# First layer of a two-layer block: turns inside the tile stream, gates ahead of queries, dot products for the late adaptive rows, step sizes with tokens on the partitions

## The chip, the cores and the metric

The kernel runs on one core of a Trainium2 chip. The metric is the device time of one execution in microseconds. The engines are TensorE (PE, with its weight loads listed as PEld), VectorE (DVE), ScalarE (ACT), GpSimd (POOL) and SyncE (SP, which only issues DMAs here). All data are float32. A large product is made of three passes: every weight and every activation is split into a rounded high part and a low part (w_hi, w_lo, h_hi, h_lo), and PE adds hi x hi, hi x lo and lo x hi.

## The reference

One sequence of 512 tokens of width 1024 passes through two layers. The first has a neighbourhood attention and a state-space scan side by side; the second has a windowed attention. The change touches the first layer up to its attention. Cut to what matters:

```python
mod = silu(c) @ ada_w + ada_b                      # 6 rows of 1024: sh1, sc1, g1, sh2, sc2, g2
h = rms_norm(x, norm1_w) * (1 + sc1) + sh1         # hc likewise, from 256 context tokens
p = h @ w_in                                       # q, k, v (512 columns each), z, xs (512), B, C (256), dt (16)
q, k = axial_rope(q), axial_rope(k)
attn = neighbourhood_attention(q, k, v, kc, vc, rpb, rows)    # 8 heads, key windows and all context keys
dt = softplus(p_dt + dt_bias)                      # per token, 2 directions x 8 heads
xs, B, C = silu(depthwise_conv(...))               # three taps along the tokens
y = ssd_bidirectional(z, xs, B, C, dt, -exp(a_log), ...)      # needs xs and B with tokens on the partitions
x = x + g1 * (concat([attn, y]) @ w_out)
x = x + g2 * conv_glu(rms_norm(x, norm2_w) * (1 + sc2) + sh2, ...)
```

g1, sh2, sc2 and g2 are the late adaptive rows: they are needed only behind the attention and the scan.

## The kernel before, in words

Weights come in blocks of 1 MB (128 partitions x 2048). For each block SP issues the load into w_raw (two buffers), ACT copies it to w_hi (`high`), POOL subtracts to get w_lo (`low`, four instructions), and PE multiplies. The order on every engine is written out by hand, and semaphores join the engines.

The projection `p = h @ w_in` is a stream of 24 output tiles of 128 columns, two to a block, in the order of `KINDS`: k (tiles 0 to 3), v (4 to 7), xs (8 to 11), B (12, 13), C (14, 15), q (16 to 19), z (20 to 23). Tile n uses the PSUM bank n mod 4. PE may begin tile n when tile n-4 has been taken out of its bank (`tile_free`) and the block's low part is there (`lo_done`). The first 14 tiles have a second part for the 256 context tokens (`ctx_product`, plain float32, from w_raw, in banks 4 and 5). `lead` makes tiles 0 to 3 as the pieces of h become ready (`h_low`).

A k tile is rotated by DVE (`rope`), and the last of these is followed by a small row `brow` of the second layer's bias, made from bank 7 (`brow_done`, `brow_sb`). A v tile is copied out by DVE. For xs, B and C, ACT writes the middle tap, DVE adds the outer taps (`outer_taps`), and ACT takes silu; then the same for the context part. For q, DVE does five instructions that read the bank and two that add. For z, ACT takes silu. Beside each of the tiles 4 to 19 DVE multiplies one 1 MB chunk of ada_w by a value per partition and adds it to a sum (`add_ada1`, 128x2048); the chunks go through a ring of two, which ACT refills between its own instructions (`load_ada`, which waits until DVE has used a chunk).

Three serial parts stand between the last tile and the attention. PE sums the collected ada rows over the partitions (32 products with a column of ones, line 1223). The step sizes dt are worked out on 16 partitions x 768 columns by DVE and ACT (lines 1535 to 1541 and 1840 to 1854). Then 19 groups of four transposes (`TR`, line 1246) bring v, the context v, xs and B to tokens on the partitions: a v window is first gathered by DVE (line 1863), PE turns the group, and ACT and DVE copy groups out in turn (lines 1551 and 1881). After the eleventh group come the turns of dt and three small sums (lines 1234 to 1240). Then the attention begins: 16 steps G of scores for two heads (lines 494, 495), largest value and bias on DVE, exp on ACT, scaling on POOL (line 610), transposes on PE (line 504), copies on ACT (line 551), and weighing of v (line 515). Before it, POOL has made the low parts of blocks 12 and 13, the first two of the output projection.

## Time and profile before

| | |
|---|---|
| median of 3 runs | 1487.64 us (1487.33 to 1490.51) |
| the profiled execution's own time | 1488.21 us |
| its span, first to last instruction | 1486.4 us |
| PE busy | 1385.2 us (93%) |
| DVE, ACT, POOL busy | 603.2, 567.3, 636.4 us |
| mean granted TensorE clock over the span | 0.963 of full speed |
| share of the chain that ended last | PE 81%, DVE 6%, POOL 5%, issue 3%, ACT 3% |

The span leaves out 1.8 us of the execution. A busy PE is not a PE at its peak: the granted clock says in which stretches it ran at half speed. The chain of waits goes back from the last instruction to whatever released each one. Two matmul records of the profile stand for one plain float32 product, and one for a transpose or a rounded product.

### The profile page before, as it was taken

To read this page: it belongs to the slowest core of one execution; us is meant where nothing else is said; L and a number is where in the kernel's file an instruction comes from. 1 tells how busy PE (TensorE), PEld (TensorE's weight loads), DVE (VectorE), ACT (ScalarE), POOL (GpSimd) and SP (SyncE) were. 2 spreads that over 40 slices of the span, in tenths; PEclk is the share of its full clock that TensorE was granted. 3 is DMA by queue.
4 is the path that set the end of the run, shared out by engine and by line. 5 is a ranking of instruction groups with operands and counts; after the bars stand their busy time and mean duration, and the time that the engine had idled before them with its cause. 6 is when DMAs were issued, how large, how long until landed. Compare 5 with 4: busy or idle time off the path is not lost.

```text
span 1486.4 us, 17325 instructions
## 1 busy us (share of the span) xinstructions
PE 1385.2 (93%) x6360; PEld 1109.6 (75%) x6360; DVE 603.2 (41%) x1088; ACT 567.3 (38%) x856; POOL 636.4 (43%) x516
## 2 busy tenths in 40 slices
PE   8899997798778899999999989999979999999997
PEld 1788866686666678888888878755668888888885
DVE  2544578576852444434354243276151000001123
ACT  3512313463322534444333352377454222222331
POOL 0243354134642254444556654433523445445563
PEclk9899998899979899999999989999989999999999
DMA  9224552700012054454442242200211232322321
GB/s 394 93 101 162 214 188 98 170 1 1 1 57 113 29 220 176 184 211 178 189 155 99 88 168 85 86 1 1 70 44 57 85 113 85 107 90 85 113 85 57
DMA packets 26981, 165.49 MB, mean 111 GB/s; under 512 B 2688, under 2 KB 4992, under 8 KB 8496
## 3 DMA queue, kind: packets, MB, share of 16 engines
q1 hardware_dynamic: 24912, 150.10, 27.7%
q10 hardware_dynamic: 2016, 14.68, 2.8%
q8 instruction: 34, 0.56, 0.2%
q14 instruction: 19, 0.16, 0.0%
HBM read 162.64 MB, written 6.32 MB: 114 GB/s over the span
## 4 chain that ended last, share of the span: by engine, by line
PE 81%; DVE 6%; POOL 5%; issue 3%; ACT 3%; DMA 1%; SPq 0%; ACTq 0%; DVEq 0%; POOLq 0%
PE bank L271 48%; PE bank L335 9%; PE bank L312 5%; PE bank L1186 3%; PE bank L654 2%; PE bank L634 2%; PE bank L515 2%; POOL arena L832 1%; POOL w_lo L264 1%; PE bank L1163 1%; DMA w_raw<-w_dram 1%; POOL arena L834 1%; PE bank L1246 1%; PE bank L644 1%; PE bank L494 1%
## 5 line engine op out<-in xcount | busy, mean ns | idle before, releaser
L264 POOL TENSOR_TENSOR w_lo<-w_raw,w_hi 128x512 fp32r<-128x512 f32 x356 | 486.7, 1398 | 639.9 <-ACT w_hi L255 635.5
L271 PE MATMUL bank<-h_hi,w_hi 128*128 128x512 f32 x1120 | 445.2, 397 | 19.6 <-POOL w_lo L264 9.8
L271 PE MATMUL bank<-h_lo,w_hi 128*128 128x512 f32 x1120 | 440.3, 393 | 0.0
L271 PE MATMUL bank<-h_hi,w_lo 128*128 128x512 f32 x1120 | 439.8, 393 | 0.0
L255 ACT ACTIVATE w_hi<-w_raw 128x2048 fp32r<-128x2048 f32 x89 | 170.5, 1915 | 408.2 <-PE bank L271 189.5
L271 PEld LDWEIGHTS bank<-h_hi,w_hi 128*128 128x128 f32 x1120 | 213.5, 191 | 65.9 <-issue 13.7
L271 PEld LDWEIGHTS bank<-h_hi,w_lo 128*128 128x128 f32 x1120 | 212.9, 190 | 45.0
L271 PEld LDWEIGHTS bank<-h_lo,w_hi 128*128 128x128 f32 x1120 | 213.3, 190 | 43.6
L2036 DVE TENSOR_TENSOR arena<-arena,bank 128x512 f32 (+1 forms) x22 | 15.1, 688 | 210.2 <-PE bank L271 210.2
L1908 DVE TENSOR_TENSOR h_lo<-arena,h_hi 128x1024 fp32r<-128x1024 f32 x22 | 32.8, 1503 | 136.9 <-ACT h_hi L1585 125.4
L1753 DVE SCALAR_TENSOR_TENSOR arena<-bank,params,arena 128x511 f32<-128x511 f32 (+1 forms) x36 | 25.4, 705 | 147.2 <-ACT arena L1565 114.5
L335 PE MATMUL bank<-w_hi,h_hi 128*128 128x512 f32 x192 | 74.9, 390 | 4.7 <-POOL arena_rounded L232 3.3
L335 PE MATMUL bank<-w_hi,h_lo 128*128 128x512 f32 x192 | 75.0, 390 | 0.0
L335 PE MATMUL bank<-w_lo,h_hi 128*128 128x512 f32 x192 | 75.0, 390 | 0.0
L1744 DVE CUSTOM_DVE_ANT_0 ada_ring<-ada_ring,arena 128x1024 f32<-128x1024 f32 x48 | 62.2, 1331 | 0.0
L790 POOL TENSOR_SCALAR arena<-arena,small 128x256 f32<-128x256 f32 (+1 forms) x64 | 32.8, 532 | 55.6 <-DVE small L748 55.6
L610 POOL TENSOR_SCALAR arena<-arena,small 128x512 f32<-128x512 f32 x32 | 21.7, 692 | 73.2 <-DVE small L589 73.2
L1186 PE MATMUL bank<-arena,w_raw 128*128 128x256 f32 x224 | 50.5, 379 | 0.0
L1186 PEld LDWEIGHTS bank<-arena,w_raw 128*128 128x128 f32 x224 | 42.4, 190 | 6.9 <-issue 0.9
L634 PE MATMUL bank<-arena 128*128 128x256 f32 (+1 forms) x128 | 44.2, 458 | 3.5 <-DVE ada_ring L1992 2.6
L335 PEld LDWEIGHTS bank<-w_hi,h_hi 128*128 128x128 f32 x192 | 36.2, 188 | 13.4 <-issue 3.7
L312 PE MATMUL bank<-h_hi,w_hi 128*128 128x512 f32 x112 | 43.7, 390 | 0.0
(262 smaller groups left out, 1881.7 us busy)
## 6 DMA issues: line engine op xcount, KB each, us to landing
w_raw<-w_dram SPq DMA_DIRECT2D x92, 1024.0 KB, 4.8
ada_ring<-ada_dram SPq DMA_DIRECT2D x30, 1024.0 KB, 4.8
ada_ring<-ada_dram ACTq DMA_DIRECT2D x14, 1024.0 KB, 4.9
arena<-ada_dram SPq DMA_DIRECT2D x4, 1024.0 KB, 10.5
arena<-x_dram SPq DMA_DIRECT2D x2, 2048.0 KB, 11.4
bias_copies<-bias_rows SPq DMA_DIRECT2D x1, 4096.0 KB, 26.6
arena<-bias_copies SPq DMA_DIRECT2D x1, 3072.0 KB, 13.5
out_dram<-arena SPq DMA_DIRECT2D x8, 256.0 KB, 2.1
```

Of the source, the lines that this page charges most:

```text
L255: nc.scalar.activation(w_hi[b % 2][:], w_raw[b % 2][:], ACT.Copy).then_inc(hi_done, 1)
L264: last = nc.gpsimd.tensor_tensor(w_lo[b % 2][:, part], w_raw[b % 2][:, part], w_hi[b % 2][:, part], ALU.subtract)
L271: last = nc.tensor.matmul(bank[:, :], w[:, ft, k, :], x[:, k, :], start=k == first and m == 0, stop=k == final and m == 2)
L312: last = nc.tensor.matmul(ps[f][:, :], w[:, k, f, :], x[:, 2 * gslot + k, :], start=bank_free is not None and k == 0 and m == 0, stop=False)
L335: last = nc.tensor.matmul(ps[2 * t + h][:, :], x[:, slot + k, part], w[n][:, k, cols], start=start and m == 0, stop=stop and m == 2)
L515: last = nc.tensor.matmul(ps[7][:, 0:256], v, pt1[G % 2][:, kb, :], start=kb == 0, stop=kb == 3)
L634: nc.tensor.matmul(ps[u % 3][:, 0:128 * (hi - lo)], q2[:, 2 * g + hq // 2, t * 128:(t + 1) * 128], k2[:, g, hq % 2, lo * 128:hi * 128], st ...
L654: last = nc.tensor.matmul(ps[7][:, :], vtok2[:, lo + kb, g, :], pt2[:, G % 2, kb, :], start=kb == 0, stop=kb == hi - lo - 1)
L790: nc.gpsimd.tensor_scalar(prob2[:, u % 8, 0:w], prob2[:, u % 8, 0:w], row_inv[:, u % 16:u % 16 + 1], 1.0, ALU.mult, ALU.mult).then_inc(s[" ...
L1186: last = nc.tensor.matmul(ps[4 + n % 2][:, 0:CTX], raw[:, n % 2, k, :], HC[:, k, :], start=k == 0, stop=k == DC - 1)
L1744: last = nc.vector.tensor_tensor_reduce(out=src, in0=src, in1=row2, scale=1.0, scalar=0.0, op0=ALU.mult, op1=ALU.add, accum_out=dots[:, 2 ...
L1908: nc.vector.tensor_tensor(h_lo[:, slot:slot + 2, :], HID[:, chunk, :], h_hi[:, slot:slot + 2, :], ALU.subtract)\
```

## The change

Seven edits, all in the first layer:

1. `KINDS`: z is now tiles 16 to 19 and q is 20 to 23.
2. The 19 turn groups are spread behind the tiles 8 to 19 by the table `TR_AFTER`, in banks 6 and 7, and ACT copies all of them out. v is no longer copied and gathered by DVE: ACT writes the four key windows straight from the bank (four instructions of 128x256 a tile). The loops over tiles are written out.
3. Late adaptive rows: ada_w is laid out transposed, a row of silu(c) is spread over the partitions once (8 products on PE, two copies on DVE, inside the first stage), and every chunk takes two dot products with a summed output (128x1024). Two chunks are used beside each of the tiles 4 to 11. The 32 products with ones are gone.
4. Step sizes: the raw dt is turned first (6 transposes behind tile 16), and DVE and ACT work on 128 x 96 beside the z tiles; the sums come behind tile 19.
5. q: ACT copies the four swapped quarters out of the bank (`rot_done`), and DVE has two full-width products and the two adds.
6. The scores of attention step 0 stand before tile 23, and the rest of the attention behind it. POOL makes the low part of block 13 in four pieces between its scalings 6 to 18. The attention's transposes use the same banks 3 to 6 in another order (`TURN1`).
7. PE waits for `brow_sb` before tile 4, and not only before dt. SP issues the loads of rpb, the mask and the 4 MB `bias_copies` between block 10 and block 11, and not behind block 15. ACT no longer waits for the tenth state before its first scan exponents.

```diff
-    + [("b", 0), ("b", 1), ("c", 0), ("c", 1)] + [("q", j) for j in range(4)] + [("z", j) for j in range(4)]
+    + [("b", 0), ("b", 1), ("c", 0), ("c", 1)] + [("z", j) for j in range(4)] + [("q", j) for j in range(4)]
...
+        TR_AFTER = {8: (0, 1), 9: (2, 3), 10: (4, 5), 11: (6, 7), 12: (8, 9), 13: (10, 11), 16: (12, 13), 17: (14, 15), 18: (16, 17), 19: (18,)}
+        TURN1 = (4, 5, 6, 3)
...
@@ sync
-            for b in range(4, 14):
+            for b in range(4, 11):
                 load_block(sp, b, wait_pe=b - 2 < 7)
-            for b in (14, 15):
-                load_block(sp, b)
             sp.wait_ge(ada_used, 24)
             for r in range(ROWS):
...
             sp.dma_start(copies_dram, src).then_inc(copies_out, 16)
+            for b in range(11, 16):
+                load_block(sp, b)
@@ tensor
+            for k in range(DC):
+                last = nc.tensor.matmul(ps[2 + k // 4][:, k % 4 * P:(k % 4 + 1) * P], silu_c[:, k, 0:1].to_broadcast([P, P]), ident,
+                                        start=True, stop=True)
+            last.then_inc(row1_done, 1)
...
+            def turn_group(k):
+                if k >= 2:
+                    pe.wait_ge(tr_out, k - 1)
...
+            pe.wait_ge(brow_sb, 1)
+            for n in range(4, 23):
                 w_in_tile(n, ctx=n < N_CTX)
-            for f in range(32):
-                last = nc.tensor.matmul(ps[4][:, f:f + 1], acc1[:, f * 128:(f + 1) * 128], ones[:, 0:1], start=True, stop=True)
+                for k in TR_AFTER.get(n, ()):
+                    turn_group(k)
+                if n == 15:
+                    dt_products()
+                elif n == 16:
+                    turn_dt()
+                elif n == 19:
+                    dt_sums()
             pe.wait_ge(bias_in, 16 * 9)
-            attention1_pe(pe)
+            pe.wait_ge(tile_free, 22)
+            attention1_pe(pe, range(1))
+            w_in_tile(23, ctx=False)
+            pe.wait_ge(tile_free, 23)
+            pe.wait_ge(tr_out, N_TR)
+            pe.wait_ge(sd["wend"], 2)
+            attention1_pe(pe, range(1, NG + 2))
@@ scalar
-                if 5 <= n < 19:
-                    load_ada(act, T["ada1"][n + 5], n + 5)
+                if n == 5:
+                    load_ada(act, T["ada1"][10], 10)
+                if 5 <= n < 12:
+                    load_ada(act, T["ada1"][2 * n + 1], 2 * n + 1)
+                if kind == "v":
+                    for t in range(4):
+                        last = nc.scalar.activation(v_win[t][:, j, :].rearrange("p (r c) -> p r c", r=ROWS),
+                                                    tokens(ps[n % 4][:, :], KEY_COL[t], 32), ACT.Copy)
...
+                if kind == "q":
...
+                    for q in range(4):
+                        to, of = slice(32 * q, 32 * q + 32), slice(32 * (q ^ 1), 32 * (q ^ 1) + 32)
+                        last = nc.scalar.activation(tmp[to, 2 + n % 2, :], ps[n % 4][of, :], ACT.Copy)
+                    last.then_inc(rot_done, 1)
+                for k in TR_AFTER.get(n, ()):
+                    act.wait_ge(tr_done, k + 1)
+                    nc.scalar.activation(TR[k][1], ps[6 + k % 2][:, :], ACT.Copy).then_inc(tr_out, 1)
                 if n % 2:
                     high(act, n // 2 + 2)
+                if 5 <= n < 11:
+                    load_ada(act, T["ada1"][2 * n + 2], 2 * n + 2)
+                if kind == "q" and j == 1:
+                    act.wait_ge(sd["col"], 1)
+                    nc.scalar.activation(wend, tmp48, ACT.Exp).then_inc(sd["wend"], 1)
+                    nc.scalar.activation(cdec[:, :], ps[5][:, 96:192], ACT.Exp).then_inc(sd["wend"], 1)
+                if kind == "q" and j == 2:
+                    attention1_act(act, range(1))
@@ vector, add_ada1
-                    nc.vector.scalar_tensor_tensor(out=dst, in0=src, scalar=by, in1=dst, op0=ALU.mult, op1=ALU.add)
+                for f in range(2):
+                    at, src = 2 * (c - 8) + f, ada[:, s * BLK + f * D:s * BLK + (f + 1) * D]
+                    last = nc.vector.tensor_tensor_reduce(out=src, in0=src, in1=row1, scale=1.0, scalar=par_("adab")[:, 16 + at:17 + at],
+                                                          op0=ALU.mult, op1=ALU.add, accum_out=modb[:, at:at + 1])
...
+                if n == 22:
+                    dve.wait_ge(bias_in, 16 * 9)
+                    attention1_dve(dve, range(1))
```

On PE, at the start of tile 4 (L1200 and L1217 are the product behind `brow`, L1186 and L1203 the context part), this stood before:

```order
L1200 MATMUL bank<-arena,params 16x512 [waits con2_in]
L1201 UNCONDITIONAL_BRANCH
L1201 ISA
L1193 ISA [waits tile_free]
L1182 REGISTER_ALU [waits lo_done]
```

and now this:

```order
L271 MATMUL bank<-h_hi,w_lo 128x512
L1217 MATMUL bank<-arena,params 16x512 [waits con2_in]
L1203 MATMUL bank<-arena,w_raw 128x256 [waits lo_done,ctx_free,tile_free,brow_sb]
L1203 MATMUL bank<-arena,w_raw 128x256 x7
L271 MATMUL bank<-h_hi,w_hi 128x512
```

The product behind `brow` stays where it was, and tile 4 has one more wait.

On PE, between the last tile and the attention, this stood before (L1223 the sums of ada rows, L1246 turn groups, L1234 to L1240 dt, L494 scores):

```order
L1223 MATMUL bank<-constants,arena 128x1 x32
L1246 MATMUL bank<-constants,arena 128x128 x44
L1234 MATMUL bank<-constants,arena 128x16 x12
L1238 MATMUL bank<-small,constants 128x48
L1239 MATMUL bank<-small,constants 128x48
L1240 MATMUL bank<-small,constants 128x96
L1246 MATMUL bank<-constants,arena 128x128 x32
L494 MATMUL bank<-arena 128x256
```

and now, behind tile 23 (L498, L499 scores, L510 the attention's transposes, L521 weighing):

```order
L271 MATMUL bank<-h_hi,w_lo 128x512
L498 MATMUL bank<-arena 128x256 [waits ssd_wend,tr_out,tile_free]
L499 MATMUL bank<-arena 128x256
L498 MATMUL bank<-arena 128x256 [waits att1_probs]
L499 MATMUL bank<-arena 128x256
L510 MATMUL bank<-constants,arena 128x128 [waits att1_norm]
L510 MATMUL bank<-constants,arena 128x128 x3
L510 MATMUL bank<-constants,arena 128x128 [waits att1_norm]
```

Nothing but the attention is left there.

On ACT, from tile 21 to the attention's start (L1583 the quarters of q, L255 `high`, L1596 and L1597 the exponents of the state weights, L549 the attention's exp), it is now:

```order
L1583 ACTIVATE arena<-bank 32x512 [waits tap_silu,tile_free,half_used]
L1583 ACTIVATE arena<-bank 32x512 x3
L255 ACTIVATE w_hi<-w_raw 128x2048 [waits half_used,raw_in0]
L1596 ACT_TABLE_LOAD
L1596 ACTIVATE small<-small 128x96 [waits ssd_col]
L1597 ACTIVATE chunk_decay<-bank 128x96
L1583 ACTIVATE arena<-bank 32x512 [waits tap_silu,tile_free,half_used]
L1583 ACTIVATE arena<-bank 32x512 x3
L549 ACTIVATE arena,small<-bank,small 128x512 [waits att1_nmax] x2
L1583 ACTIVATE arena<-bank 32x512 [waits tap_silu,tile_free,half_used]
L1583 ACTIVATE arena<-bank 32x512 x3
L255 ACTIVATE w_hi<-w_raw 128x2048 [waits half_used,raw_in1]
```

The exponents of attention step 0 stand between the quarters of tile 22 and those of tile 23.

## Rows read from the trace of the kernel before

**Rows 1.** Stretches: us; busy PE, PEld, DVE, ACT, POOL; clock, DMA share, GB/s
```profile
193.40:239.60 46.20, 44.55 (x196) 35.78 (x195) 35.91 (x38) 9.61 (x11) 20.96 (x12) 1.00 0.41 151
239.60:277.60 38.00, 25.07 (x164) 23.17 (x162) 27.32 (x52) 13.86 (x18) 12.34 (x8) 0.69 0.62 146
277.60:357.00 79.40, 73.69 (x384) 61.74 (x384) 51.87 (x178) 49.94 (x131) 22.33 (x33) 0.98 0.11 36
```
**Rows 2.** Chain of waits, last tile to attention: start us, us, what
```profile
270.25 0.85 PE bank L1234 x12
...
272.44 3.51 PE bank L1246 x32
...
288.58 1.99 PE bank L515 x8
...
291.45 0.43 PE bank L494 x2
```
**Rows 3.** Chain of waits, tile 9
```profile
139.38 3.45 PE bank L1186 x16
142.83 5.45 PE bank L271 x24
```
**Rows 4.** PE in order of time, tile 20 and behind tile 23
```profile
218.66 0.50 PE L271 MATMUL bank<-h_hi,w_hi 128*128 128x512 f32 x1 [1.65 <-POOL w_lo L264]
...
240.60 9.18 PE L1223 MATMUL bank<-constants,arena 128*128 128x1 f32 x64
```
**Rows 5.** DVE in order of time, last k tile and brow
```profile
84.81 0.69 DVE L1786 SCALAR_TENSOR_TENSOR arena<-bank,arena 128x512 f32<-128x512 f32 x1 [3.97 <-PE bank L271]
...
89.06 0.68 DVE L1834 TENSOR_TENSOR arena<-bank,arena 16x512 f32<-16x512 f32 x1
```
**Rows 6.** PE in order of time, start of tile 4
```profile
85.66 2.64 PE L1186 MATMUL bank<-arena,w_raw 128*128 128x256 f32 x11
```
**Rows 7.** PE in order of time, two instructions behind a gap
```profile
47.10 0.77 PE L271 MATMUL bank<-h_hi,w_hi 128*128 128x512 f32 x1 [3.16 <-DVE h_lo L1775]
...
1456.23 0.47 PE L335 MATMUL bank<-w_hi,h_hi 128*128 128x512 f32 x1 [3.29 <-POOL arena_rounded L232]
```
**Rows 8.** Stretches behind those gaps, columns as in Rows 1
```profile
47.00:51.00 4.00, 3.90 (x9) 3.14 (x10) 4.00 (x4) 3.97 (x6) 0.00 (x0) 0.51 0.02 4
...
1458.00:1462.00 4.00, 4.00 (x13) 3.08 (x12) 0.15 (x1) 0.69 (x2) 0.00 (x0) 0.67 0.00 0
```
**Rows 9.** Two source lines of DVE: least/median/most ns, first and last start us
```profile
L1744 DVE CUSTOM_DVE_ANT_0 ada_ring<-ada_ring,arena x48: 1211/1218/2311, 519.7 to 802.3; 128x1024 f32<-128x1024 f32 x48
...
L1798 DVE TENSOR_TENSOR arena<-arena x8: 684/756/1686, 204.3 to 231.1; 64x512 f32<-64x512 f32 x8
```
**Rows 10.** ACT in order of time, two copies out of banks and a `high`
```profile
239.53 1.28 ACT L1546 ACT_TABLE_LOAD   x1
240.82 1.08 ACT L1546 ACTIVATE arena<-bank 128x512 f32<-128x512 f32 x2
241.79 1.91 ACT L255 ACTIVATE w_hi<-w_raw 128x2048 fp32r<-128x2048 f32 x1
```
**Rows 11.** DVE in order of time, last context tap behind tile 8
```profile
143.73 0.48 DVE L1755 SCALAR_TENSOR_TENSOR arena<-bank,params,arena 128x255 f32<-128x255 f32 x1
```
**Rows 12.** DMA issues: count, KB each, median us to landing
```profile
w_raw<-w_dram SPq DMA_DIRECT2D x92, 1024.0 KB, 4.8
...
bias_copies<-bias_rows SPq DMA_DIRECT2D x1, 4096.0 KB, 26.6
```
**Rows 13.** DVE in order of time, attention steps 0 and 1
```profile
280.32 0.43 DVE L579 TENSOR_TENSOR bank<-bank,ada_ring 128x256 f32<-128x256 f32 x1 [1.66 <-PE bank L495]
...
284.11 0.17 DVE L589 RECIPROCAL small<-small 128x2 f32<-128x2 f32 x1 [0.84 <-ACT arena L543]
```
**Rows 14.** POOL and PE in order of time, a steady attention step
```profile
314.41 1.36 POOL L610 TENSOR_SCALAR arena<-arena,small 128x512 f32<-128x512 f32 x2 [3.07 <-DVE small L589]
...
316.98 1.04 PE L504 MATMUL bank<-constants,arena 128*128 128x128 f32 x8
```

331 lines of the change are left out of this document (163 added, 168 removed).

## The prediction

> **What bounds the kernel now.** I read the stretches first, then the chain of waits, then the engines in order of time where the chain changes hands. The 24 tiles are bound by PE: while the last eight are made, PE is busy for 44.55 of 46.2 us at a granted clock of 1.00, and DVE, with 35.9 us, is next [rows 1]. The following 38.0 us are different: PE has 25.1 us of work in them and a clock of 0.69 [rows 1]. That is the serial part (sums of the ada rows, dt, turns). The attention then fills PE for 73.7 of 79.4 us at 0.98 [rows 1]. So the question is how much of the part between tile 23 and the attention goes, and what PE, the bound before and behind it, gets to do instead.
>
> Tile 23 ends at 240.60, where the product with ones begins [rows 4], and the first weighing of v, from which the attention keeps its steady pace, is at 288.58 [rows 2]. The difference, 48.0 us, is what the change works on.
>
> **The change part by part, in terms of PE's time.**
>
> *The serial part goes: -48.0 us.* The 9.18 us of products with ones [rows 4], the dt chain and the gathering of v fall away or move beside tiles. What is late next is the start of the attention behind tile 23. The last queries set it, by way of ACT and DVE:
>
> - ACT copies four quarters of a bank, 0.54 us each by the pair in 1.08 us, so 2.2 us [rows 10].
> - DVE then has two full-width products, 0.69 us each (the first is the same as now [rows 5], the second I take as equal), and two adds, 0.69 us each at their shortest [rows 9]: 2.8 us.
> - Behind tile 21 ACT has 2.2 us of quarters, 1.9 us of `high`, a table load of 1.28 us [rows 10] and two small exponents of about 0.25 us: 5.9 us, against the 5.45 us of tile 22 [rows 3]. It is 0.5 us late for tile 22.
> - Then come 2.2 us of quarters and 2.8 us of DVE, with 0.6 us more because POOL is making block 12's low part (the adds take 0.68 to 1.69 us [rows 9]). Then step 0's largest values and exponents, 3.8 us from 280.32 to 284.11 [rows 13]. Only then do the quarters of tile 23 follow, 2.2 us, and their 2.8 us on DVE. From the reciprocal of step 0 to the first weighing it is 4.5 us, 284.11 to 288.58 [rows 2, 13].
>
> Together 19.4 us from the end of tile 22. PE spends 1.7 us of them on the first scores (four products of 0.43 us [rows 2]), up to 0.2 us on waiting, and 5.45 us on tile 23. That leaves 12.0 us behind tile 23, in which PE is idle for about 7 us. The gaps of 3.16 and 3.29 us [rows 7] were followed by stretches of 4 us at 0.51 and 0.67 of the full clock [rows 8], which cost 2.0 and 1.3 us. I add 1.5 us: **13.5 us** in place of 48.0.
>
> *A stall goes: -1.65 us.* PE waited for POOL before tile 20 [rows 4]. In the new stream more time passes between blocks, so the low part is early.
>
> *Turns in the stream: +16.7 us.* 19 groups at 0.88 us, from the four groups in 3.51 us at a clock of 1.00 [rows 2]. PE is the bound there, so all of it counts. Their copies (19 x 0.54 us on ACT [rows 10]) lie beside the tiles.
>
> *dt: +1.4 us.* The twelve small turns and the sums took 2.2 us, 270.25 to 272.44 [rows 2]. Six turns go, 0.4 us, and so does the wait between them, 0.4 us. The dt products move, but cost the same. The chain on 128 x 96 lies beside the z tiles.
>
> *First scores: +1.7 us* before tile 23; they are in the 13.5 us no more.
>
> *The new wait for `brow_sb`: +4.1 us, and +1.7 us of clock.* Tile 4 began at 85.66 [rows 6]. DVE takes up the last k tile at 84.81 and has `brow` at 89.06 + 0.68 = 89.74 [rows 5], and nothing in the change makes it earlier. Behind PE's wait stands the whole stream, with three free banks that are of no use now. By rows 7 and 8 the idle 4.1 us also bring the clock to its lower level; bounds 0 (the gap of 1.65 us in rows 4 lies in a stretch at 1.00) and 2.0 us (rows 8), taken 1.7.
>
> *The row of silu(c): -0.8 us.* 8 products of 0.21 us at full clock (half of a 256-column product, 3.45 us over 8 [rows 3]) or 0.43 us at half clock fit into the 3.16 us before 47.10 [rows 7], at worst 0.3 us too long. They keep PE at work there, which may give back part of the 2.0 us that the low clock cost from 47 to 51 [rows 8], though h comes in pieces. Bounds +0.3 and -1.4.
>
> *The stream's other engines: +1.5 us.* For tiles 8 to 11 PE takes 3.45 + 5.45 [rows 3] + 1.76 = 10.7 us. DVE is done with the taps 4.8 us behind a tile's end (143.73 + 0.48 against 139.38 [rows 3, 11]) and then has four dot products of 1.22 us [rows 9] and as many reads of the sum at 0.08 us, 5.2 us: 10.0 us, just under. In every second tile POOL makes a low part; if that stretches four dot products to 2.31 us, the longest seen [rows 9], DVE falls back 3 us per pair of tiles, 6 us by tile 11. The group's copies on ACT, which waits for DVE at every `load_ada`, may be about 4.7 us late before PE waits (6 us against 10.7 us). I take 1.5 us; bounds 0 and the rival below. For tiles 4 to 7 DVE has 5.6 us of 8.9 us.
>
> The Trainium skill (SBUF — State Buffer, section "Who interferes with whom") says that a DVE instruction with two SBUF inputs and a GpSimd instruction that reads SBUF block each other for a whole instruction. The dot product is of that kind, and the spread from 1211 to 2311 ns [rows 9] agrees; by the rule only those beside a low part are hit, which is the case above and not the rival below.
>
> *POOL's pieces in the attention: +0.4 us.* Scaling ends at 315.77 and the turns begin at 316.98 [rows 14], 1.2 us of room for a piece of 1.3 us, four times. Bounds 0 and 1.6.
>
> *At nothing:* v windows on ACT (four copies a tile, ACT is the emptiest engine there), the order of z before q, the ACT wait taken out of the scan.
>
> Sum: -48.0 + 13.5 - 1.65 + 16.7 + 1.4 + 1.7 + 4.1 + 1.7 - 0.8 + 1.5 + 0.4 = -9.45 us. The profiled execution took 1488.2 us (span 1486.4 and 1.8 around it), 0.6 us above the median. So 1478.8 us on its own scale, **1478.2 us** against the median of 1487.64.
>
> **The rivals.**
>
> *Everything is hidden (more gain).* No low clock behind the `brow` wait (1.7) or at the attention's start (1.5), the full 1.4 us in the first stage (0.6), no delay by DVE (1.5) or POOL (0.4): 5.7 us less, 1472.5 us. For it: the gap in rows 4 left the clock alone. Against it: rows 7 and 8.
>
> *Block 11 is late.* The 4 MB copy now stands in SP's queue ahead of blocks 11 to 15. It took 26.6 us [rows 12]. Counted from the end of tile 13, block 8's low part is ready at some 13.5 us, the copy is issued at about 18, and block 11 behind it lands at about 48. PE reaches tile 22 at 62 us (two tiles, dt with 24 x 0.23 + 8 x 0.43 = 9.0 us by rows 3, four tiles with turns, two more), and `high` and `low` need 8 us, so it must be there by 54. If the load of rpb and the weights slow the copy by 11 us, PE waits 5 us: 1483 us.
>
> *DVE becomes the bound, and the gain is lost.* If all dot products take 2.31 us, DVE needs 4.8 + 4 x 2.39 = 14.4 us per tile against 10.7 for tiles 8 to 11 and 10.0 against 8.9 for tiles 4 to 7: 19 us behind at tile 11, less 4.7 us of room and the 1.5 us counted: 1491 us. For it: DVE is close to its limit and ACT waits for it twice a tile. Against it: the median is 1.22 us, and POOL makes only one low part for two tiles.
>
> *Slower: the turns let the clock fall.* If PE's clock fell to its lower level behind each of the ten turn stretches, as behind the gaps of rows 7, at 1.7 us each, it would be 17 us more: 1495 us. It decides if the turns do not count as work. Against it: the attention runs at 0.98 [rows 1] with a turn of two groups in each step, and the four groups of rows 2 ran at full speed. The Trainium skill (TensorE: Matmul & The Clock Gate, section "Part 4: PE-mode transpose") says that transposes do not bring the clock up; rows 1 show that between other products they do not bring it down.
>
> **How the numbers follow.** The forecast has 0.66, more gain 0.12, block 11 late 0.09, DVE the bound 0.08, the clock 0.05. A measurement of this kernel can tell 0.2%, 3 us, from no change: faster is below 1484.7 and slower above 1490.6. Faster: 0.66 + 0.12 + 0.07 of the late block = 0.85. The DVE case is split, 0.05 within and 0.03 above, so 0.07 the same with the rest of the late block, and 0.08 slower. The range of 1472.5 to 1484.5 us takes in the first two cases and most of the third. Its ends are those of the bounds: everything hidden below; above, the forecast with 5 to 6 us from a late block or a DVE that falls back further.
>
> **What the profile after would show.** PE idle for about 4 us before tile 4, ended by DVE, and a granted clock near half behind it. Tiles 8 to 11 about 10.7 us apart, with PE at 1.00 throughout; a wait of PE for ACT in a turn group, or for POOL, would be the DVE case. No wait for POOL at tile 22, else block 11 was late. Tile 23 ending near 265, and about 12 to 14 us from there to the first weighing, PE waiting for POOL's scaling. An attention of the same pace as before. The forecast is wrong if the idle time behind tile 23 is above 17 us, or if `brow` is ready when PE arrives.

## The result and the profile after

The changed kernel takes 1468.83 us (median of 4 runs, 1468.02 to 1470.08) against 1488.43 us (4 runs) for the kernel before: ratio 0.9866, 95% interval 0.9846 to 0.9886. In a second session the same kernel had a ratio of 0.9892 (0.9871 to 0.9914). The forecast was 1478.2 us with a range of 1472.5 to 1484.5 us. The direction was right and the size was not: the gain is 19.6 us, about twice the 9.45 us forecast, and the time lies outside the range on the fast side.

The profiled execution took 1470.08 us, its span is 1468.3 us and its mean clock 0.969 (before: 0.963). First the stretches of it, with the columns of rows 1: tiles 4 to 8, tiles 9 to 15 with their turns, tiles 16 to 23 with dt, turns and first scores, the restart (from the end of tile 23 to the first weighing), and the attention behind its first weighing. The 9.1 us between the second and the third row are the dt products.

```profile
88.80:136.10 47.30, 47.27 (x202) 39.67 (x203) 23.79 (x36) 10.31 (x19) 14.39 (x9) 0.95 0.48 182
136.10:196.90 60.80, 60.80 (x298) 51.60 (x296) 37.06 (x59) 28.46 (x43) 19.53 (x15) 1.00 0.53 205
205.99:257.12 51.13, 50.13 (x242) 41.55 (x242) 17.23 (x34) 26.04 (x38) 16.49 (x13) 1.00 0.65 188
257.12:269.11 11.99, 5.88 (x25) 4.99 (x24) 6.89 (x19) 8.03 (x15) 2.64 (x4) 0.72 0.02 9
269.11:343.80 74.69, 70.40 (x373) 58.66 (x371) 50.18 (x163) 45.17 (x118) 30.41 (x39) 1.00 0.04 15
```

The 38.0 us at a clock of 0.69 that stood in rows 1 are gone. What is left of them is the fourth row, 12 us with 5.9 us of PE work. The 60.8 us of tiles 9 to 15 have no PE gap at all, and the clock is 1.00 with the turns in them. DVE's dot products, the group that answers rows 9 (busy us, mean ns, idle before them and what ended it):

```profile
L1778 DVE CUSTOM_DVE_ANT_0 ada_ring<-ada_ring,arena,params 128x1024 f32<-128x1024 f32 x32 | 42.3, 1368 | 10.6 <-DMA ada_ring<-ada_dram 10.6
```

Now the chain of waits (start us, us, what), from the end of tile 8 to the end of tile 9. It answers rows 2 and 3:

```profile
136.10 0.87 PE bank L1231 x8
136.98 3.46 PE bank L1203 x16
140.43 5.48 PE bank L271 x24
145.91 0.87 PE bank L1231 x8
```

L1231 is the transpose of a turn group. Eight instructions take 0.87 us. A group has four transposes, so one group takes 0.44 us.

The wait for `brow_sb`, from PE in order of time, and the stretch behind it (busy PE, clock, DMA share, GB/s). They answer rows 6 to 8:

```profile
88.83 6.17 PE L1203 MATMUL bank<-arena,w_raw 128*128 128x256 f32 x16 [4.06 <-DVE arena L1918]
```
```profile
84.80:89.00 4.20, 0.17 (x1) 0.76 0.72 252
89.00:93.00 4.00, 4.00 (x10) 0.50 0.04 8
```

And the restart, all engines in order of time, from the end of tile 23 (257.12) to the first weighing. It answers rows 2 and 13:

```profile
257.12 0.59 PE L498 MATMUL bank<-arena 128*128 128x256 f32 x2
257.45 0.49 DVE L588 CUSTOM_DVE_ANT_1 bank<-bank,ada_ring,small 128x256 f32<-128x256 f32 x1
258.04 0.69 ACT L549 ACTIVATE arena<-bank,small 128x512 f32<-128x512 f32 x1 [0.45 <-DVE small L588]
258.84 2.38 ACT L1583 ACTIVATE arena<-bank 32x512 f32<-32x512 f32 x4
261.25 1.91 ACT L255 ACTIVATE w_hi<-w_raw 128x2048 fp32r<-128x2048 f32 x1
261.36 0.69 DVE L1836 SCALAR_TENSOR_TENSOR arena<-bank,arena 128x512 f32<-128x512 f32 x1 [3.35 <-ACT arena L1583]
264.10 0.17 DVE L595 RECIPROCAL small<-small 128x2 f32<-128x2 f32 x1
264.36 1.36 POOL L616 TENSOR_SCALAR arena<-arena,small 128x512 f32<-128x512 f32 x2 [11.06 <-DVE small L595]
265.11 1.97 PE L510 MATMUL bank<-constants,arena 128*128 128x128 f32 x8 [6.11 <-POOL arena L616]
...
269.11 1.24 PE L521 MATMUL bank<-arena 128*128 128x256 f32 x5
```

Read it backwards: PE waits 6.11 us for POOL's scaling, POOL for the reciprocal, and the reciprocal stands on DVE behind the rope of tile 23, which waited 3.35 us for ACT's quarters. Those stand behind the exponents of step 0. The exponent sum of step 0, all that the reciprocal needs, was there at about 258.8, over five microseconds before it was used.

In the chain the first weighing begins at 269.27, against 288.58 in rows 2: 19.3 us earlier. The two spans differ by 18.1 us. The rest is not a cost of the change that the runs could pin down: the scan (from 338.0 to the output projection at 419.86) took 81.9 us in this execution and 80.0 us in the second one of the same kernel; before it was 81.2 us.

### The profile page after: what moved, and what is told of

Same layout as the page of the kernel before. It is cut to its first block, busy times and chain, and to the rows that moved or that the text cites. A ratio compares the mean times of both kernels' runs of the same rounds, so it can differ in the third digit from the quotient of the medians.

```text
span 1468.3 us, 17191 instructions
## 1 busy us (share of the span) xinstructions
PE 1376.2 (94%) x6306; PEld 1099.9 (75%) x6306; DVE 572.7 (39%) x1080; ACT 583.6 (40%) x897; POOL 626.0 (43%) x516
## 4 chain that ended last, share of the span: by engine, by line
PE 84%; POOL 5%; DVE 4%; ACT 3%; issue 2%; DMA 1%; SPq 0%; ACTq 0%; DVEq 0%; POOLq 0%
PE bank L271 51%; PE bank L335 9%; PE bank L312 5%; PE bank L1203 3%; PE bank L668 2%; PE bank L648 2%; PE bank L521 2%; POOL arena L846 1%; POOL w_lo L264 1%; PE bank L1176 1%; DMA w_raw<-w_dram 1%; PE bank L510 1%; POOL arena L848 1%; PE bank L658 1%; PE bank L498 1%
## 5 line engine op out<-in xcount | busy, mean ns | idle before, releaser
L264 POOL TENSOR_TENSOR w_lo<-w_raw,w_hi 128x512 fp32r<-128x512 f32 x352 | 471.3, 1370 | 652.9 <-ACT w_hi L255 652.9
L271 PE MATMUL bank<-h_hi,w_hi 128*128 128x512 f32 x1120 | 445.4, 398 | 16.0 <-POOL w_lo L264 8.1
L255 ACT ACTIVATE w_hi<-w_raw 128x2048 fp32r<-128x2048 f32 x89 | 170.5, 1916 | 365.9 <-PE bank L271 189.6
L1203 PE MATMUL bank<-arena,w_raw 128*128 128x256 f32 x224 | 53.0, 392 | 4.1 <-DVE arena L1918 4.1
L1203 PEld LDWEIGHTS bank<-arena,w_raw 128*128 128x128 f32 x224 | 43.8, 198 | 11.4 <-DVE arena L1918 5.0
L1778 DVE CUSTOM_DVE_ANT_0 ada_ring<-ada_ring,arena,params 128x1024 f32<-128x1024 f32 x32 | 42.3, 1368 | 10.6 <-DMA ada_ring<-ada_dram 10.6
```

Of the source, the lines that this page charges most:

```text
L255: nc.scalar.activation(w_hi[b % 2][:], w_raw[b % 2][:], ACT.Copy).then_inc(hi_done, 1)
L264: last = nc.gpsimd.tensor_tensor(w_lo[b % 2][:, part], w_raw[b % 2][:, part], w_hi[b % 2][:, part], ALU.subtract)
L271: last = nc.tensor.matmul(bank[:, :], w[:, ft, k, :], x[:, k, :], start=k == first and m == 0, stop=k == final and m == 2)
L1203: last = nc.tensor.matmul(ps[4 + n % 2][:, 0:CTX], raw[:, n % 2, k, :], HC[:, k, :], start=k == 0, stop=k == DC - 1)
L1778: last = nc.vector.tensor_tensor_reduce(out=src, in0=src, in1=row1, scale=1.0, scalar=par_("adab")[:, 16 + at:17 + at], op0=ALU.mult, op1= ...
```

## The experiments

Each is the changed kernel with one edit, unless said otherwise. Below, "first scores" is the start of step 0's scores, behind tile 22: what the tile stream gained or lost before it can be read there to a tenth of a microsecond. The changed kernel has 249.84 in its first profile and 248.65 in its second. "The scan" is the start of the scan's first products on PE, behind the attention.

The expectations and the text use these short names: e1_brow_late is the kernel with the moved wait for `brow_sb`, e6_rope_behind the one with the reciprocal ahead of the last rope, e6h_rope_high the same with the high part of block 13 later, e7_no_dots the one without dot products, e8_both the one with both ends together, and e9_late_turns the last one.

### The changed kernel again

> The changed kernel once more, as the base for the runs of the same call. It was 19.6 us faster than before (1468.8 against 1488.4). Expected again: 0.9866 of before within 0.2%, 19 turn groups of 0.44 us each (8.3 us on PE), PE idle for 4.05 us before tile 4 and for 6.1 us behind tile 23.

1470.39 us (4 runs), 0.9892 of before. The wait for `brow_sb` left PE idle for 4.07 us and the restart for 6.11 us, as in the first profile. The context part of tile 4 took 5.15 us here and 6.17 there: how long the clock stays low behind the wait is not the same each time.

The same holds for the restart. Here the first scores come 1.2 us earlier than in the first profile, and the first weighing at the same time (269.28 against 269.27). Both executions are idle for 6.11 us and then turn eight blocks in 1.97 us; the eight score records behind them take 3.36 us here and 2.19 us there. So the restart took 13.3 us in this execution and 12.15 us in the first. Eight executions of this study leave the restart as it is in the changed kernel; from their first scores to the scan they take 88.2 to 89.5 us. A gain that is read at the first scores can therefore be larger or smaller by up to 1.3 us at the scan.

### The wait for brow_sb moved to where the bank is written

```diff
-            pe.wait_ge(brow_sb, 1)
             for n in range(4, 23):
...
+                if k == 1:
+                    pe.wait_ge(brow_sb, 1)
```

> PE's wait for brow_sb stands before the second turn group (the first writer of bank 7) and not before tile 4. Theory: the wait holds the whole stream, and it costs its 4.05 us of idle PE and 2.7 us of low clock behind it (the context part of tile 4 took 6.17 us instead of 3.45): 6.8 us less than the changed kernel, some 1462 us, tile 4 starting near 84.8 at a clock of 1.00. Rival: another wait takes its place (a bank, a low part, or the ring of late adaptive rows that DVE and ACT serve): then 0 to 3 us less. Second rival, the idle time alone counts and the clock comes down anyway: 4.1 us less.

1462.7 us, ratio to before 0.9839 (0.9820 to 0.9857). PE in order of time, and the stretches (PE, clock):

```profile
83.60 1.03 PE L1217 MATMUL bank<-arena,params 32*16 32x512 f32 x2
84.56 3.72 PE L1203 MATMUL bank<-arena,w_raw 128*128 128x256 f32 x16
```
```profile
84.80:89.00 4.20, 4.20 (x20) 1.00 0.60 238
89.00:93.00 4.00, 4.00 (x19) 1.00 0.04 8
```

The context part ends at 88.28 instead of 95.00, and the first scores stand at 243.10 instead of 249.84: 6.7 us in both places, so nothing took the wait's place over eighteen tiles. (Some 0.15 us of it was there ahead of the wait: L1217 starts at 83.60 here and at 83.75 in the changed kernel.) The theory holds with its number at the first scores. At the scan 5.4 us of it are left (332.60 against 338.01 and 338.08), because the low clock of this execution's restart lasted as long as in the second profile of the changed kernel. The wait costs time where it stands, and it has no need to.

### PE kept at work ahead of that wait

```diff
+            for m in range(17):
+                nc.tensor.matmul(ps[6][:, :], h_hi[:, 0, 0:128], h_hi[:, m % 8, :], start=True, stop=True)
             pe.wait_ge(brow_sb, 1)
```

> 17 products of no use (128x512, 3 to 4 us together) are given to PE ahead of the wait for brow_sb, so that it isn't idle there. The wait itself stays. If the lower clock behind the wait comes from the idle time, the context part of tile 4 goes back from 6.17 to 3.45 us: 2.7 us less than the changed kernel, some 1466 us. The rival, that the clock there comes from something else (the smaller width of the context products, or what was before the wait), expects no change, 1468.8 us, or up to 0.5 us more where the products outlast the wait.

1466.28 us, 0.9865 (0.9845 to 0.9885). PE in order of time:

```profile
84.74 4.15 PE L1259 MATMUL bank<-h_hi 128*128 128x512 f32 x17
88.88 3.72 PE L1203 MATMUL bank<-arena,w_raw 128*128 128x256 f32 x16
```

Tile 4 begins at the same time as with the wait (88.88 against 88.83), but its context part takes 3.72 us and the clock is 1.00. The first scores come 2.4 us earlier than in the first profile of the changed kernel and 1.2 us earlier than in the second. So the wait costs 4.1 us of idle time and, in these two executions of the changed kernel, 1.4 and 2.4 us of low clock behind it (5.15 and 6.17 us against 3.72), 6.5 us in the first; work that computes nothing buys the second part back.

### Every turn group twice

```diff
+                for _ in range(2):
                     for m, src in enumerate(TR[k][0]):
                         last = nc.tensor.transpose(ps[6 + k % 2][:, m * 128:(m + 1) * 128], src, ident)
```

> Each turn group in the tile stream issues its four transposes twice, 76 more transposes and no other work. The theory that four transposes of 128x128 take 0.44 us in the stream (0.11 us each at full clock) expects 8.3 us more than the changed kernel, some 1477 us. The forecast's size of a group, 0.88 us, would be 16.7 us more, 1485.5 us. If the clock fell because of transposes, tiles behind them would show a clock under 1.00, and it would be more still.

1477.12 us, 0.9941 (0.9922 to 0.9960), 6.7 us over the second session's run of the changed kernel. From the chain and from PE in order of time:

```profile
136.48 1.75 PE bank L1232 x16
138.23 3.46 PE bank L1203 x16
141.69 5.48 PE bank L271 x24
```
```profile
258.52 0.67 PE L498 MATMUL bank<-arena 128*128 128x256 f32 x2 [0.99 <-DVE arena L1851]
```

The first scores are 8.68 us later than in the first profile; 0.37 us of it was there already at the end of tile 4's context part (95.37 against 95.00). 8.31 us for 76 more transposes are 0.109 us each, 0.44 us a group. The forecast's size would have put them at 266.5. The clock stayed at 1.00 through all of them.

### The turns in two lumps

```diff
-        TR_AFTER = {8: (0, 1), 9: (2, 3), 10: (4, 5), 11: (6, 7), 12: (8, 9), 13: (10, 11), 16: (12, 13), ...}
+        TR_AFTER = {13: tuple(range(12)), 19: tuple(range(12, 19))}
```

> The same 19 turn groups, but in two lumps: twelve behind tile 13 and seven behind tile 19. Theory: spread out, a group costs PE its 0.44 us and the copy on ACT (0.59 us, one group behind, two banks) is hidden by the tiles; in a lump the copies set the pace and ACT must first finish its taps of that tile. Then PE waits for ACT: some 5 us in the first lump, 1.5 us in the second, perhaps 1 to 2 us of low clock behind it: 5 to 8 us more than the changed kernel, 1474 to 1477 us. Rival: it doesn't matter where the groups stand, 1468 to 1470 us.

1482.27 us (10 runs), 0.9963 (0.9948 to 0.9978). PE in order of time:

```profile
173.81 3.69 PE L1203 MATMUL bank<-arena,w_raw 128*128 128x256 f32 x16 [0.91 <-DVE arena L1799]
...
189.65 7.80 PE L1231 MATMUL bank<-constants,arena 128*128 128x128 f32 x40 [5.78 <-ACT arena L1589]
```

The first two groups of the lump were done at 183.8. Then PE waited for ACT, which had the taps of tiles 12 and 13 before it (in the stream these lie beside the products). Behind that gap of 5.78 us the granted clock was 0.50 up to 193.5 and 0.95 from there on: first PE was the slower one, with about 0.9 us a group while ACT waited for each, and then the groups came 0.67 us apart. The lump took 14.6 us (182.83 to 197.45) where twelve groups in the stream take 5.3. The first scores came at 262.65, 12.8 us late, more than the 5 to 8 us expected. The direction holds; I had counted the taps of one tile on ACT, and there were two, because those of tile 12 had waited on DVE for the dot products before them. The first row shows something else: without turn groups beside the tiles 8 to 11 a tile takes PE 8.9 us, less than DVE's 10 us, and then PE does wait for DVE's taps (0.45 us at 163.7, 0.91 us at 173.8). Spreading the groups is worth more than moving them into the stream as a block would be.

### Step 0 of the attention behind tile 23

```diff
-            attention1_pe(pe, range(1))
             w_in_tile(23, ctx=False)
...
-            attention1_pe(pe, range(1, NG + 2))
+            attention1_pe(pe, range(NG + 2))
```
(and the same on ACT and DVE)

> Step 0 of the attention (its scores, largest values and exponents) stands behind tile 23 on PE, DVE and ACT, as the rest does. If the scores ahead of tile 23 shorten the start of the attention, as the change has it, taking them away costs 1 to 3 us against the changed kernel. The other reading of its trace: ACT's two exponents stand ahead of the quarters of tile 23 and wait for DVE, so the early step 0 delays the last rope by some 4 us, and nothing is won: without it PE also loses the 0.99 us of waiting before the scores; the first weighing then comes 0 to 1.5 us earlier, 1467.5 to 1469 us.

1469.58 us, 0.9871 (0.9837 to 0.9905). All engines in order of time:

```profile
255.29 0.70 PE L498 MATMUL bank<-arena 128*128 128x256 f32 x2
257.99 0.69 DVE L1833 SCALAR_TENSOR_TENSOR arena<-bank,arena 128x512 f32<-128x512 f32 x1 [2.75 <-ACT arena L1582]
264.28 0.17 DVE L595 RECIPROCAL small<-small 128x2 f32<-128x2 f32 x1 [0.85 <-ACT arena L549]
...
269.15 1.03 PE L521 MATMUL bank<-arena 128*128 128x256 f32 x4
```

The first weighing is at 269.15, where it was at 269.11. The early step 0 wins nothing as it is written: it starts its exponents early, they push the last quarters and rope back by 3.4 us on ACT and DVE (257.99 against 261.36), and the reciprocal comes at the same time.

### The reciprocal ahead of the last rope

```diff
                     attention1_dve(dve, range(1))
+                    dve.wait_ge(sd["wend"], 3)
+                    attention1_dve(dve, range(1, 2))
...
-            dve.wait_ge(sd["wend"], 3)
-            attention1_dve(dve, range(1, NG + 2))
+            attention1_dve(dve, range(2, NG + 2))
@@ scalar, the copy of a turned group
+                if u == 0:
+                    act.wait_ge(tile_free, 24)
```

> DVE works out the reciprocal of step 0 and the largest values of step 1 before the rope of tile 23 instead of behind it (ACT's first copy of a turned group then waits for that rope, since it writes over its buffers). In the changed kernel DVE was idle for 3.35 us there, waiting for the quarters of tile 23, while POOL's scaling of step 0 waited for the reciprocal. Theory: the first turns start some 5 us earlier and the first weighing 2.6 us earlier (then ACT's high part of block 13 and its exponents set it): 1466.2 us. Rival: the last rope is itself the end of the chain, and nothing changes.

1466.23 us, 0.9840 (0.9803 to 0.9878). All engines in order of time:

```profile
259.17 0.17 DVE L597 RECIPROCAL small<-small 128x2 f32<-128x2 f32 x1 [0.91 <-ACT arena L549]
260.19 1.32 PE L510 MATMUL bank<-constants,arena 128*128 128x128 f32 x8 [0.94 <-POOL arena L618]
261.51 1.91 ACT L255 ACTIVATE w_hi<-w_raw 128x2048 fp32r<-128x2048 f32 x1
264.27 0.70 PE L498 MATMUL bank<-arena 128*128 128x256 f32 x2 [1.89 <-ACT arena L549]
265.92 3.32 PE L521 MATMUL bank<-arena 128*128 128x256 f32 x8 [0.45 <-ACT arena L559]
```

The gap of 6.11 us before the turns is 0.94 us now, and the weighing starts 3.2 us earlier, but takes 3.32 us instead of 1.89, at a granted clock of 0.57. The scan begins at 336.24 instead of 338.01: with the 0.25 us by which this execution was late at the first scores, 2.0 us won of the 2.6 expected. That is against the quickest restart of the changed kernel: from the first scores to the scan it is 86.15 us here, and 88.2 to 89.5 us there. ACT is the next in line: its `high` of block 13 stands before the exponents of step 1, and PE waits 1.89 us for them.

### And the high part of block 13 later

```diff
-                if n % 2:
+                if n % 2 and n < 23:
                     high(act, n // 2 + 2)
...
-            attention1_act(act, range(1, NG + 2))
+            attention1_act(act, range(1, 3))
+            high(act, 13)
+            attention1_act(act, range(3, NG + 2))
```

> As e6_rope_behind, and the high part of block 13 (1.9 us on ACT) stands behind the attention's step 2 instead of before step 1. If ACT sets the start there, the first weighing comes another 0.7 us earlier (3.3 us against the changed kernel, 1465.5 us). The rival is that ACT lacks those 1.9 us in the attention and gives them back there: no difference to e6_rope_behind or worse.

1465.07 us, 0.9844 (0.9810 to 0.9878). The scan begins at 334.68, 3.3 us earlier than in the changed kernel and 3.5 us with the late start of this execution taken off, where 3.3 were expected. But only part of the step from 2.0 to 3.5 us is the work of `high`. From the first scores to the first weighing it is 15.46 us, where e6_rope_behind has 15.83: 0.4 us, of 0.7 expected. The rest is in the clock behind it. The same restart stands in e8_both below, and the first weighing there, behind a gap of the same length, ran at 0.56 of full speed. The first row is of this kernel, the second of e8_both:

```profile
265.42 1.99 PE L521 MATMUL bank<-arena 128*128 128x256 f32 x8 [2.08 <-ACT arena L559]
```
```profile
259.72 3.41 PE L521 MATMUL bank<-arena 128*128 128x256 f32 x8 [2.07 <-ACT arena L559]
```

From the first scores to the scan it is 84.72 us here and 86.13 us in e8_both, no less than in e6_rope_behind. So what stands in front of step 0's reciprocal is shown to set the restart. What stands in front of step 1's exponents is next, but it is worth 0.4 us, and the other 1.0 us of this execution can't be counted on.

### Without the dot products, and without the row of silu(c)

```diff
-                for f in range(2):
-                    last = nc.vector.tensor_tensor_reduce(out=src, in0=src, in1=row1, ...)
-                last.then_inc(ada_used, 1)
+                nc.vector.tensor_copy(modb[:, at:at + 2], par_("adab")[:, 16 + at:18 + at]).then_inc(ada_used, 1)
```
(the second also without the eight products and DVE's two copies of the row)

> The 32 dot products of the late adaptive rows are left out: a copy of two columns stands in their place, so the chunks of ada_w are loaded and released but the product with silu(c) is missing from the rows. Theory: DVE was idle at times beside the tiles 4 to 11 and PE had no gap there, so DVE's backlog is 0 us: the time of the changed kernel, PE at tile 8's end at the same place within 0.2 us. The forecast's term expects 1.5 us less, the rival in which DVE is the bound more than that.

> As e7_no_dots, and the eight products that spread silu(c) over the partitions and DVE's two copies of them are left out of the first stage as well (nothing reads the row then). Theory: they keep PE at work before the first pieces of h, and without them the low clock of the kernel before is back between 47 and 51 us: tile 3 ends 0.9 us later than with them, though DVE has 1.4 us less to do. Rival: the clock there isn't their doing; then it stays at 1.00 and the time is the same or up to 0.5 us less.

1469.68 us (0.9886, 0.9854 to 0.9918) without the dot products. DVE's work between 88.8 and 136.1 falls from 23.79 to 7.59 us, and PE doesn't notice: tile 8 ends at 136.15 (136.10 with them), and the first scores come at 249.88 (249.84). The row is of the kernel without dot products, columns as in rows 1:

```profile
88.80:136.10 47.30, 47.30 (x202) 39.64 (x203) 7.59 (x12) 10.59 (x19) 15.28 (x11) 0.94 0.54 199
```

DVE's backlog costs the changed kernel 0 us, and the rival in which DVE is the bound is out.

Without the row as well: 1470.82 us (0.9896, 0.9864 to 0.9927). The stretches from 43 to 51 us (PE, clock), first without the dot products alone, then without the row too:

```profile
43.00:47.00 4.00, 4.00 (x20) 0.59 0.36 145
47.00:51.00 4.00, 2.85 (x12) 1.00 0.00 0
```
```profile
43.00:47.00 4.00, 0.84 (x4) 0.56 0.30 120
47.00:51.00 4.00, 4.00 (x13) 0.58 0.00 0
```

The low clock of rows 8 is back, so it was the eight products that took it away. They are worth 0.4 us behind tile 3 (PE comes to the wait for `brow_sb` at 84.61 against 85.03), not 0.9: with a full clock PE then waits 1.15 us for the next piece of h, which limits what the clock can give. The other 0.5 us by which tile 3 ended earlier than before is in how early the first piece of h came (46.29 without the row, 47.10 in rows 7), and that is not the row's doing. It is the clock once more: behind a gap of 2.10 us at 41 us the small products ahead of h (L1174 and L418) ran at a granted clock of 0.50 in the kernel before and took 3.0 us, and at 1.00 in the kernel without the row, 1.8 us. Both then wait 3.16 us for h. It isn't the change's doing either: e8_both, which is the changed kernel in this stage, has the clock of 0.50 there as well. So this half microsecond can come or stay away with the same code; how often it does in the kernel before is not known from its one profile.

### Both ends together

The edits of the moved `brow_sb` wait and of the two restart experiments in one kernel.

> e1_brow_late and e6h_rope_high together. They stand at two ends of the stream and share no engine time, so their gains should add: about 6 us and 4 us less than the changed kernel, first weighing near 259.7 us, 1458.5 us in all. Rival: with the stream earlier, block 12 or 13, or the bias copies that land in it, come late for the attention's start, and part of the 10 us is lost.

1460.39 us, 0.9823 (0.9792 to 0.9855), 8.4 to 10.0 us under the two medians of the changed kernel, in another session, and 1.9 us more than expected. The first weighing is at 259.72, where 259.7 was expected. The scan begins at 330.40, 7.6 us earlier than in the changed kernel; the two kernels with one end each had 5.4 and 3.3. The 1.1 us that are missing from their sum lie ahead of every edit. In the first stage PE begins the small products ahead of h 0.9 us later than in e1_brow_late (41.96 against 41.07) and runs them at 0.50, and it has tile 3 behind it 1.15 us later. So the gains do add, but at the scan they add up to 8.7 us and not to 10. PE's idle times between tile 3 and the first weighing are 0.98, 0.92 and 2.07 us, and none is for a block, so the rival (a late block or late bias copies) did not come.

### And two turn groups in the restart

```diff
-        TR_AFTER = {..., 17: (14, 15), 18: (16, 17), 19: (18,)}
+        TR_AFTER = {..., 17: (14, 15), 18: (16,)}
+        TR_LATE = (17, 18)
@@ attention, PE, behind the scores of step 1 (ACT copies them out behind step 1's exponents)
+                if G == 1:
+                    for k in TR_LATE:
+                        pe.wait_ge(tr_out, k - 1)
+                        for m, src in enumerate(TR[k][0]):
+                            last = nc.tensor.transpose(ps[6 + k % 2][:, m * 128:(m + 1) * 128], src, ident)
```

> e8_both, and two of the 19 turn groups (those of bT) stand behind the scores of step 1, where PE is idle, instead of behind the tiles 18 and 19, where it is the bound. PE gets 0.44 us for each in the stream: 0.9 us less than e8_both. Their two copies (0.6 us each) fall between ACT's exponents and its first copy of a turned group, where it waits for the last rope. Rival: ACT has no room there, and the first weighing keeps its place or comes 0.3 us later against the end of tile 23.

1458.27 us, 0.9808 (0.9774 to 0.9842), the fastest kernel of the study. All engines in order of time:

```profile
236.30 0.47 PE L271 MATMUL bank<-h_hi,w_hi 128*128 128x512 f32 x1 [0.27 <-POOL w_lo L264]
242.48 0.67 PE L499 MATMUL bank<-arena 128*128 128x256 f32 x2 [0.47 <-DVE arena L1867]
251.47 1.04 PE L538 MATMUL bank<-constants,arena 128*128 128x128 f32 x8
252.58 1.32 PE L511 MATMUL bank<-constants,arena 128*128 128x128 f32 x8
256.80 1.08 ACT L568 ACTIVATE arena<-bank 128x512 f32<-128x512 f32 x2 [0.47 <-DVE arena L1867]
258.02 2.81 PE L522 MATMUL bank<-arena 128*128 128x256 f32 x8 [2.16 <-ACT arena L568]
```

L538 are the two late groups; they lie in idle time and their copies before a wait. The scores of step 1 come 7.3 us behind those of step 0 as before, and the way from the first scores to the scan is as long as in the kernel before it (86.15 us from 242.48, against 86.13 us from 244.27). From the end of the product behind `brow` to the first scores it is 0.9 us less, so in these two executions the whole of the 0.9 us stays. It is less than the medians of four runs can confirm (they differ by 2.1 us, with spreads of 3 to 4 us), and 0.9 of the 1.8 us between the two profiles is the first stage again.

The first row shows the next limit: tile 22 waits 0.27 us for the low part of block 11. The earlier the stream gets there, the longer ACT waits for that block's load: 1.30 us in the changed kernel, 2.70 us in e1_brow_late, 2.90 us in e8_both and 3.53 us here. By this row of numbers a still shorter stream waits for the block.

## Why the forecast was wrong, point by point

The sum of the forecast, and the same sum with what the profile after shows. Behind tile 22 the forecast counted the restart, the first scores, a wait of 0.2 us and tile 23 (20.9 us together); the trace has 20.4 us. (The 0.2 us were taken off the part behind tile 23 and never added as a term, a slip that changes nothing here.)

| term | forecast, us | measured, us | from |
|---|---|---|---|
| serial part goes | -48.0 | -48.0 | rows 2, 4 |
| restart behind tile 23 | +13.5 | +12.15 | chain, 257.12 to 269.27; 13.3 in the second execution |
| first scores, with the wait before them | +1.7 | +2.7 | 0.99 us of waiting for the rope's add |
| turns in the stream | +16.7 | **+8.3** | chain; every group twice |
| dt | +1.4 | +1.1 | 6 transposes 0.47, sums 0.64 |
| `brow_sb`, idle and clock | +5.8 | +6.5 | wait moved, PE kept at work |
| stall at tile 20 | -1.65 | -1.65 | no gap there |
| row of silu(c), first stage | -0.8 | -0.9 | PE at `brow`'s product 83.75 against 84.70; the row's own part 0.4 |
| stream's other engines | +1.5 | 0 | dot products left out |
| POOL's pieces | +0.4 | not seen | see below |
| sum | -9.45 | -19.8 | first weighing: -19.3 |

The 0.5 us between the measured terms and the first weighing have not been followed further.

**The step that failed is "19 groups at 0.88 us, from the four groups in 3.51 us".** The row says `L1246 x32`. A product in plain float32 leaves two records and a transpose one, as the section on the profile before says, so x32 are 32 transposes, eight groups, not four. I read the count as if it were the products'. The total could have told it: the group of that line has 76 transposes in the kernel before, and 19 groups of four are 76. Of the 10.35 us between the two sums this one term is 8.4. The experiment with every group twice settles it against the value that I used.

**DVE's backlog (+1.5) cost nothing.** The sum was right that DVE has about 10 us of work in a period of 10.7 (with the smaller groups 9.8 us). What was missing is what PE needs of it: only the taps that free a bank, and there are four banks. That reading is argued from the order on the engines; the experiment shows the 0 us. It holds for a stream with turns: with the turns taken out from beside these tiles, PE waited for the taps (0.45 and 0.91 us). The dot products took 1273 to 2292 ns with a median of 1280, and DVE even waited 10.6 us for chunks of ada_w; the slow ones stayed its own affair.

**The restart was sized well and explained half right.** It took 12.15 us and, in a second execution, 13.3 us, where I gave 13.5. I followed ACT's quarters and the rope, as the trace has it. I did not ask whether the reciprocal needs to stand behind them; it doesn't, and moving it won 2.0 us or more. Nor does the early step 0 shorten anything as it is written in the change, which the forecast took for a gain: without it the first weighing stands at the same time.

**The `brow_sb` wait was right in place, order and nearly in size**: 4.1 us idle as forecast, and 2.4 us of clock, where 1.7 was taken between bounds of 0 and 2.0. The upper bound was too low: over nine executions with the wait, the context part of tile 4 took between 5.15 and 6.78 us, against 3.72 without it. The Trainium skill (TensorE: Matmul & The Clock Gate, section "Why this matters for your kernels") advises against idle gaps of PE between bursts of matmuls, from a certain length on; the 4.1 us here agree. At the restart with the reciprocal early no gap was longer than 1.89 us, under that length, and the weighing behind them still ran at a granted clock of 0.57 (3.32 us), so there shorter gaps were no safety.

**The turns and the clock.** The rival in which the turns bring the clock down is out: through 60.8 us with twelve turn groups it is 1.00, and with twice as many too.

**Block 11** was not late: PE has no wait for POOL's low parts at tile 22. The forecast had its landing at about 48 us behind the end of tile 13, and ACT takes it up at 48.8 us. By the forecast's own terms PE reaches tile 22 at 60.2 us and not at 62; it did at 58.4 us, and the low part was there some 2.5 us before. So the rival (0.09) didn't come, but its mechanism is there: with a stream 7 to 8 us shorter, PE waited 0.27 us for that block in e9_late_turns.

**POOL's pieces and the rest of the run.** From the first weighing to the scan it is 68.7 us, against 69.0 before. The term of 0.4 us does not appear.

The range failed with the forecast: its lower end, everything hidden, was worked out from the same 16.7 us, so a misread term moved the forecast and both ends together. Bounds on the costs that were not known were no help against a cost that was thought known.

## What to carry to other kernels

Before a duration "x32" is divided into parts, find out how many instructions a part leaves in the trace, and check it with a total that is known from the code. When work is moved into the stream of the engine that is the bound, its own time is the whole price, provided that what takes its results away is spread in the same way. A wait placed early on the bound engine for the sake of a later writer costs its idle time and the clock behind it; put it before that writer. At a restart, look for the short instruction (here a reciprocal of 0.17 us) that stands in program order behind a long one it doesn't need. And read a gain at more than one place and in more than one execution: behind an idle gap the low clock moved the same restart by up to 1.3 us.

## What the runs showed of the hardware

- A 128x128 float32 transpose takes 0.109 us of PE in a sequence at a clock of 1.00 (272 ns from start to modelled end), and 0.22 us behind a gap, where the clock is half (eight in 1.97 us with the overlap, against 1.04).
- The same gap of 4.06 us was followed by 5.15 to 6.78 us for the same eight float32 products over nine executions. The low clock behind a gap has no fixed length.
- Short gaps give either clock. Gaps of 0.93 and 2.07 us in the same restart were followed by a granted clock of 1.00 in one execution (the first weighing in 1.99 us) and of 0.56 in another (3.41 us).
- A DVE copy of 128x2 took 4.03 us once and 0.16 us as a rule. It began at 95.4 us, beside the end of a low part on POOL, and ended at 99.4 us, when POOL's memset of 3.5 us ended. That POOL held it is a reading of this one coincidence; no run tried it.

From the kernel without dot products, the copy's line (least/median/most ns, first and last start), and POOL in order of time:

```profile
L1777 DVE COPY small<-params x16: 157/166/4031, 95.4 to 170.4; 128x2 f32<-128x2 f32 x16
```
```profile
95.91 3.52 POOL L1120 MEMSET arena<- 128x4096 f32 x1
```
